# Six feed-forwards of a six-layer block: high and low activations as one operand of 512 columns, halves summed on reading, up tiles of full depth

## The reference, cut to what matters

```
gu = x @ w_gate_up;  gate, up = gu[:, :FF], gu[:, FF:]          # layers 0 to 3
y  = (silu(gate) * up) @ w_down
u  = x @ ffn_w_up;   u = causal_conv(u, taps of 3, bias)        # layers 4 and 5
y  = (silu(u[:, :FF]) * u[:, FF:]) @ ffn_w_down
```

## Time and profile before

| what | value |
|---|---|
| median of 3 runs | 2353.83 us (2352.62 to 2354.62) |
| profiled execution | 2353.8 us, span 2352.0 us, mean granted clock 0.998 |
| TensorE matmul, weight load | 98%, 88% of the span, 15272 of each |
| VectorE, ScalarE, GpSimd | 62%, 56%, 14% |

### The profile page before, as it was taken

How to read it: one execution, slowest core, us unless ns; L and a number is a source line. 1 busy time by engine, 2 the same in 40 slices (tenths; PEclk the granted TensorE clock), 3 DMA queues, 4 the chain that set the end, 5 groups by cost and what they waited for, 6 DMA issues and landing times.

```text
span 2352.0 us, 36560 instructions
## 1 busy us (share of the span) xinstructions
PE 2308.6 (98%) x15272; PEld 2067.4 (88%) x15272; DVE 1453.5 (62%) x2217; ACT 1305.4 (56%) x1958; POOL 330.6 (14%) x307
## 2 busy tenths in 40 slices
PE   7999999999999999999999999999999999999999
PEld 5799978888899888998789989899899898998998
DVE  6655555546645546546764567575677686765875
ACT  5554465555544556445564467565665675655654
POOL 0100032212100313001010002343000013530000
PEclk9999999999999999999999999999999999999999
DMA  6255443333455534555345544444455453444553
GB/s 266 90 212 183 179 178 138 141 134 126 179 190 187 197 141 157 196 182 203 113 173 186 194 178 148 144 162 162 179 187 189 175 184 126 162 164 160 201 193 126
DMA packets 58180, 398.92 MB, mean 170 GB/s; under 512 B 6816, under 2 KB 7072, under 8 KB 11680
## 3 DMA queue, kind: packets, MB, share of 16 engines
q1 hardware_dynamic: 56864, 393.75, 46.7%
q10 hardware_dynamic: 1152, 2.83, 0.3%
HBM read 395.51 MB, written 1.05 MB: 169 GB/s over the span
## 4 chain that ended last, share of the span: by engine, by line
PE 82%; DVE 9%; ACT 6%; POOL 2%; issue 1%; DMA 0%; SPq 0%; ACTq 0%; DVEq 0%; POOLq 0%
PE b L1280 12%; PE b L1282 12%; PE b L1281 12%; PE b L1178 12%; PE b L1179 12%; PE b L1180 12%; PE b L1183 5%; DVE wlo L1931 4%; PE b L1187 4%; ACT whi L1581 2%; ACT b L1577 1%; DVE xb L2229 1%; PE b L1246 1%; PE b L1247 1%; ACT S L1578 1%
## 5 line engine op out<-in xcount | busy, mean ns | idle before, releaser
L1931 DVE TENSOR_TENSOR wlo<-raw,whi 128x2048 fp32r<-128x2048 f32 x362 | 845.1, 2339 | 446.4 <-ACT whi L1581 446.1
L1581 ACT ACTIVATE whi<-raw 128x2048 fp32r<-128x2048 f32 x362 | 690.5, 1913 | 426.2 <-PE b L1282 221.9
L1280 PE MATMUL b<-xh,whi 128*128 128x256 f32 x2560 | 723.9, 283 | 1.0 <-DVE wlo L1931 0.7
L1282 PE MATMUL b<-xh,wlo 128*128 128x256 f32 x2560 | 712.4, 278 | 0.0
L1281 PE MATMUL b<-xl,whi 128*128 128x256 f32 x2560 | 711.6, 278 | 0.0
L1280 PEld LDWEIGHTS b<-xh,whi 128*128 128x128 f32 x2560 | 480.3, 188 | 5.6 <-DVE wlo L1931 3.3
L1281 PEld LDWEIGHTS b<-xl,whi 128*128 128x128 f32 x2560 | 481.4, 188 | 1.9
L1282 PEld LDWEIGHTS b<-xh,wlo 128*128 128x128 f32 x2560 | 481.1, 188 | 0.0
L1178 PE MATMUL b<-whi,xh 128*128 128x512 f32 x640 | 262.9, 411 | 1.5 <-DVE wlo L1931 1.5
L1178 PE MATMUL b<-whi,oh 128*128 128x512 f32 x656 | 259.0, 395 | 0.6 <-DVE ol L2220 0.6
L1179 PE MATMUL b<-wlo,oh 128*128 128x512 f32 x656 | 256.1, 390 | 0.0
(11 more groups left out here) (238 smaller groups left out, 2904.2 us busy)
## 6 DMA issues: line engine op xcount, KB each, us to landing
raw<-in_w SPq DMA_DIRECT2D x362, 1024.0 KB, 4.8
gt<-in_rows SPq DMA_DIRECT2D x8, 512.0 KB, 4.0
bt<-in_rows SPq DMA_DIRECT2D x8, 512.0 KB, 4.9
abq<-in_rows ACTq DMA_DIRECT2D x2, 768.0 KB, 6.3
x<-in_x SPq DMA_DIRECT2D x1, 1024.0 KB, 6.6
bc<-in_rows SPq DMA_DIRECT2D x4, 256.0 KB, 5.0
out<-x SPq DMA_DIRECT2D x4, 256.0 KB, 2.0
msk<-in_masks SPq DMA_DIRECT2D x1, 768.0 KB, 21.3
```

The costliest lines, as they stand in the source:

```text
L1280: pe.matmul(out, wh[:, k, cs], ah[:, kk, :], start=kk == 0 and s == 0, stop=False, skip_group_check=True)
L1282: last = pe.matmul(out, wl[:, k, cs], ah[:, kk, :], start=False, stop=final and k == 3, skip_group_check=True)
L1581: return ac.activation(out, i, ACT.Copy)
L1931: ve.tensor_tensor(B.wlo[r][:, :], B.raw[r][:, :], B.whi[s][:, :], ALU.subtract).then_inc(sem["loV"], 1)
```

## The change

The up projection of n = 1 to 10 is rebuilt in all six feed-forwards; n = 0 stays as it was.

- A tile of up weights holds the full depth (8 blocks) for 128 columns of gate and 128 of up (`deep` in the plan), so it fills two banks alone: `up_out` writes gate and up of column tile s into banks 4, 5 (s = 0) or 6, 7 (s = 1), every round.
- xh and xl become one tile `xa`, for each block 256 columns of the high part and then 256 of the low. One matmul moves all 512 past the high weights into the whole bank; a second moves the 256 high columns past the low weights into the first half (`deep` on TensorE). The value wanted is the sum of the bank's halves.
- f < 4: VectorE sums the halves by a reduction over pairs, gate into `us`, up into `hf` (`sum_gate`, `sum_up`); silu reads `us`; a multiply follows.
- f = 4, 5: ScalarE copies the second half into `us`, VectorE adds the first (`sum_both`); taps read `us` (`tap_sum`, `taps_sum`).
- Reading goes by one column tile (`middle(n, s)`) instead of two; the transposes of n = 0 stand one yield earlier, and `unturned` stands ahead of n = 1.
- `xa` starts 8 words behind the old start of xh, all x use it, and the tiles behind it stay where they were.

```
+    def deep(name, layer, n):
+        for s in range(2):
+            plan.append(("d", name, layer, 2 * n + s))
...
-            if n < NFF:
-                cols("w_gate_up", i, [256 * n, FF + 256 * n])
+            if n == 0:
+                cols("w_gate_up", i, [0, FF])
+            elif n < NFF:
+                deep("w_gate_up", i, n)
...
+    def up_out(self, f, n, s, name, layer):
+
+        w = self.tile(("d", name, layer, 2 * n + s))
+        for part in range(2):
+            self.bank(("deep", f, n, s, part), UPS[s][part])
+            for half in range(2):
+                self.step("deep", f, n, s, part, half, w)
+                if part and half:
+                    self.gone_by_bank(w, ("deep", f, n, s, 1))
+                yield
+        self.let_go(w)
...
-
-        def middle(n, raw):
-            if raw:
-                self.step("unturned", f)
-                yield
-                yield
-                for s in range(2):
-                    self.bank(("col", ("up", f, 0), s), UPS[1][s])
-                    self.step("turned_up", f, s)
-            yield from acts(f, n)
+        acts, parts = (self.gated, self.summed) if f < 4 else (self.convolved, self.shifted)
+
+        def first():
+            yield
             for s in range(2):
-                self.counts("hhi", (f, n, s))
-                self.step("hhi", f, n, s)
-                if s:
-                    yield
+                self.bank(("col", ("up", f, 0), s), UPS[1][s])
+                self.step("turned_up", f, s)
+            yield from acts(f)
             for s in range(2):
-                self.counts("hlo", (f, n, s))
-                self.step("hlo", f, n, s)
+                self.counts("hhi", (f, 0, s))
+                self.step("hhi", f, 0, s)
+            yield
+            for s in range(2):
+                self.counts("hlo", (f, 0, s))
+                self.step("hlo", f, 0, s)
+
+        def middle(n, s):
+            yield from parts(f, n, s)
+            yield
+            self.counts("hhi", (f, n, s))
+            self.step("hhi", f, n, s)
+            yield
+            self.counts("hlo", (f, n, s))
+            self.step("hlo", f, n, s)

         for n in range(NFF + 2):
             if n == 0:
                 self.drive(self.tok_out(("up", f), up, layer, (0, FF), a, True, PAIRS[0]))
+                self.flush()
+                self.step("unturned", f)
+                self.pre.append(first())
             elif n < NFF:
-                keys = [("c", up, layer, (256 * n, FF + 256 * n), h) for h in range(2)]
-                self.drive(self.col_out(("up", f, n), keys, ("x", a), ((0, 2), (1, 3)), UPS[(n + 1) % 2]))
-            if n < NFF:
-                self.flush()
-                self.pre.append(middle(n, n == 0))
+                for s in range(2):
+                    self.drive(self.up_out(f, n, s, up, layer))
+                    self.flush()
+                    self.pre.append(middle(n, s))
...
+    def summed(self, f, n, s):
+        self.step("sum_gate", f, n, s)
+        self.counts("silu", (f, n, s))
+        self.step("silu_sum", f, n, s)
+        yield
+        self.counts("gate", (f, n, s))
+        self.step("sum_up", f, n, s)
+
+    def shifted(self, f, n, s):
+        for part in range(2):
+            self.counts("half", (f, n, s, part))
+        self.step("sum_both", f, n, s)
+        self.counts("cva", (f, n, s))
+        self.step("tap_sum", f, n, s)
+        yield
+        self.counts("cvv", (f, n, s))
+        self.step("taps_sum", f, n, s)
+        self.counts("silu", (f, n, s))
+        self.step("silu2", f, n, s)
+        yield
+        self.counts("gate", (f, n, s))
+        self.step("gate2", f, n, s)
...
+    def deep(f, n, s, part, half, w):
+        b, m = use["deep", f, n, s, part]
+        weight_ready(w)
+        source_ready(("x", 2 * f + 1), half)
+        if half == 0:
+            p.wait_ge(f"empty{b}", m)
+        wh, wl = B.deep_of(w)
+        cs = slice(128 * part, 128 * part + 128)
+        for k in range(4 * half, 4 * half + 4):
+            pe.matmul(B.bank[b][:, :], wh[:, k, cs], B.xa[:, 512 * k:512 * k + 512], start=k == 0, stop=False,
+                      skip_group_check=True)
+            last = pe.matmul(B.bank[b][:, 0:256], wl[:, k, cs], B.xa[:, 512 * k:512 * k + 256], start=False,
+                             stop=k == 7, skip_group_check=True)
+        if half:
+            last.then_inc(sem[f"full{b}"], 1)
...
+    def silu_sum(f, n, s):
+        b, m = use["deep", f, n, s, 0]
+        a.wait_ge(f"empty{b}", m + 1)
+        act(B.sg[:, s, :], B.us[:, s, :], ACT.Silu).then_inc(sem["silu"], 1)
...
+    def sum_both(f, n, s):
+        for part in range(2):
+            b, m = use["deep", f, n, s, part]
+            a.wait_ge(f"full{b}", m + 1)
+            copy(B.us[:, part, :], B.bank[b][:, 256:512]).then_inc(sem["half"], 1)
+
+    def tap_sum(f, n, s):
+        i = f - 4
+        fw, fb = B.colp(f"fw{i}"), B.colp(f"fb{i}")
+        a.wait_ge("hlo", mark["hlo", (f, n - 1, s)])
         for j, to in enumerate((B.sg, B.hf)):
             c = 22 * j + 2 * n + s
-            last = act(to[:, s, :], B.bank[b][:, 256 * j:256 * j + 256], ACT.Identity, bias=fb[:, c:c + 1],
-                       scale=fw[:, 3 * c + 2:3 * c + 3])
+            b, m = use["deep", f, n, s, j]
+            a.wait_ge(f"empty{b}", m + 1)
+            last = act(to[:, s, :], B.us[:, j, :], ACT.Identity, bias=fb[:, c:c + 1], scale=fw[:, 3 * c + 2:3 * c + 3])
         last.then_inc(sem["cva"], 1)
...
+    def add_halves(out, f, n, s, part):
+        b, m = use["deep", f, n, s, part]
+        v.wait_ge(f"full{b}", m + 1)
+        ve.tensor_reduce(out, B.bank[b][:, :].rearrange("p (h n) -> p n h", h=2), AX.X,
+                         ALU.add).then_inc(sem[f"empty{b}"], 1)
+
+    def sum_gate(f, n, s):
+        add_halves(B.us[:, s, :], f, n, s, 0)
+
+    def sum_up(f, n, s):
+        v.wait_ge("hlo", mark["hlo", (f, n - 1, s)])
+        add_halves(B.hf[:, s, :], f, n, s, 1)
+        b, m = use["deep", f, n, s, 1]
+        v.wait_ge(f"empty{b}", m + 1)
+        v.wait_ge("silu", mark["silu", (f, n, s)])
+        ve.tensor_tensor(B.hf[:, s, :], B.hf[:, s, :], B.sg[:, s, :], ALU.mult).then_inc(sem["gate"], 1)
+
+    def sum_both(f, n, s):
+        for part in range(2):
+            b, m = use["deep", f, n, s, part]
+            us = B.us[:, part, :]
+            v.wait_ge("half", mark["half", (f, n, s, part)])
+            ve.tensor_tensor(us, B.bank[b][:, 0:256], us, ALU.add).then_inc(sem[f"empty{b}"], 1)
...
+    def taps_sum(f, n, s):
+        fw = B.colp(f"fw{f - 4}")
+        v.wait_ge("cva", mark["cva", (f, n, s)])
+        for j, to in enumerate((B.sg, B.hf)):
+            c = 22 * j + 2 * n + s
+            last = convolve(to[:, s, :], B.us[:, j, :], fw[:, 3 * c:3 * c + 3], 3)
+            if j == 0:
+                last.then_inc(sem["cvv"], 1)
+            else:
+                B.tap_i = v.mine(last)
...
-        self.acts = sb("xh", [128, 2056], F32R), sb("xl", [128, 2104], F32R)
+        sb("lead", [128, 8])
+        self.xa = sb("xa", [128, 4096], F32R)
+        sb("rest", [128, 56])
...
+        self.us = self.E[2][:, :].rearrange("p (s n) -> p s n", s=2)
...
     def act(self, x):
-
-
-        places = (8, 0) if x in (0, 2, 4, 6) else (0, 24)
-        return [a[:, at:at + 2048].rearrange("p (k n) -> p k n", k=8) for a, at in zip(self.acts, places)]
+        both = self.xa[:, :].rearrange("p (k h n) -> p k h n", k=8, h=2)
+        return both[:, :, 0, :], both[:, :, 1, :]
+
+    def deep_of(self, w):
+        return [b.rearrange("p (k n) -> p k n", k=8) for b in (self.whi[w % NHL][:, :], self.wlo[w % NRAW][:, :])]
```

More of the change, by code:

```diff
@@ L146, in stream_plan @@
         for n in range(NFF + 2):
[L147 to L148 removed]
+            if n == 0:
+                cols("ffn_w_up_2", l, [0, FF])
+            elif n < NFF:
+                deep("ffn_w_up_2", l, n)
             if n >= 2:
@@ L771, in ffn, with gated, convolved @@
         finish()
-    def gated(self, f, n):
+    def gated(self, f):
         for s in range(2):
-            self.counts("silu", (f, n, s))
-        self.step("silu", f, n)
+            self.counts("silu", (f, 0, s))
+        self.step("silu", f)
         yield
-        self.step("gate", f, n)
+        self.step("gate", f)
         yield
-    def convolved(self, f, n):
+    def convolved(self, f):
         for s in range(2):
[L783 to L794, removed]
+            self.counts("cva", (f, 0, s))
+            self.step("tap", f, s)
         yield
         for s in range(2):
-            self.counts("gate", (f, n, s))
-        self.step("gate2", f, n)
-        yield
+            self.counts("cvv", (f, 0, s))
+            self.step("taps", f, s)
+        for s in range(2):
+            self.counts("silu", (f, 0, s))
+            self.step("silu2", f, 0, s)
+        yield
+        for s in range(2):
+            self.counts("gate", (f, 0, s))
```

(30 more changed lines are left out.)

41 lines of the change are left out of this document (21 added, 20 removed).

## The result

Measured: 2364.63 us median (2363.59 to 2364.85, 4 runs) against 2353.86 us for the kernel before on the same chip, ratio 1.0045, 95% interval 1.0028 to 1.0063. The forecast was 2352.3. The profiled execution's span is 2363.0 us against 2352.0, 11.0 more.

A forecast was written before the change was run, and what follows sets the result against it. It took the rate at which TensorE starts matmuls as the bound. Terms -9.0 + 5.6 - 3.3 - 0.4 + 5.6 = -1.5 us, from 2353.8 to 2352.3 us; range 2340 to 2361.

The forecast's parts named there:

- Wide operand: Up projections, rounds 1 to 10, six layers: three matmuls (351.4 ns) become a pair at 346.7 ns, gaining 9.0 us.
- rival D: Up projections: 512 columns pay the slow 233.1 ns behind a 256; loss 3.3 us instead of 9.0 won, 2364.6; chance 0.08.
- the rule weighed there: Up projections: a warm matmul takes N/2.4 + 2.5 ns, so merging two saves 2.5 ns, 4.8 us in all; total 2356.5.
- Same tile elsewhere: Second-stage mixers: streaming x loses 5.6 us, holding x stationary gains 3.3; feed-forwards' first projections gain 0.4 us.
- Reading, gated layers: Gated feed-forwards: two reductions of about 0.7 us join each half round on VectorE, hidden by TensorE, costing nothing.
- Convolution, steady state: Feed-forwards with convolution: VectorE's chain of 15.45 us a round keeps up with TensorE's 16.56, 1.1 us to spare.
- Rival C: Rounds 2 to 10 of the last two feed-forwards: VectorE's chain becomes the bound, 16 us more, 2368; chance 0.14.
- Convolution, start: First rounds of feed-forwards 4 and 5: TensorE waits for banks, 2.8 us a layer, 5.6 us for two.

The follow-up runs named there:

- groups of eight: Changed kernel with all eight 512-column matmuls of a bank first, then its eight of 256: 2354.18 us.
- early sums: Changed kernel with the sums of round 1's second half moved ahead of the first half's high and low copies, feed-forwards 4 and 5 only: 2358.88 us.
- the fastest among them: Changed kernel with sums of round 1 moved earlier and a tile's first part eight wide then eight narrow, its second the reverse: 2347.63 us.
- the tile off the grid: Changed kernel with the activation tile starting 32 bytes earlier, 32 bytes past a multiple of 64: 2360.93 us.
- narrow first: Changed kernel with the 256-column matmul before the 512-column one in each pair, lengths still alternating: 2363.9 us.
- groups of eight off the grid: Changed kernel with eight wide then eight narrow matmuls and the activation tile 32 bytes past a multiple of 64: 2367.9 us.
- groups of four: Changed kernel with four 512-column matmuls first, then four of 256, in every half of a group: 2359.23 us.
- the wide one split: Changed kernel with each 512-column matmul written as two of 256 with the same weights: 2374.51 us.

## Why the prediction was wrong, step by step

**Wide operand: the step that failed.** The pair was priced at 346.7 and measured 352.8. Both parts of the sum were right as settled intervals, but in the steady rounds neither length settles at its own: wide ones take 232 to 241, narrow ones 113 to 120. The prediction said that no row alternates them, and then took the sum of two settled rows as the middle. The size is that of rival D (353.1; its total of 2364.6 is the measured one), its mechanism in part: the wide matmuls pay 236 on the mean while narrow ones stand between them, but not always, as the pattern of 347 ns shows. The argument against D, that the down rows settle at 226.7, was true and beside the point: they have 24 matmuls to settle in. With the alternation taken out (groups of eight) a pair takes 348.3 and the kernel 2354.2. That this is near the forecast is partly luck, since the other errors below nearly cancel. The runs show that the loss shrinks as the lengths change less often; why the steady rounds fall into the dear pattern, and not into the one whose sum is the forecast 346.7, stays open. By the rule weighed there (the Trainium skill, TensorE: Matmul & The Clock Gate, "Back-to-back issue gap") a matmul's gap depends on its columns alone; here the same 512 columns measure 226.7, 233 or 241 ns. The section gives that formula for a single matmul, and for a stream with weight loads a measured 131 ns at 512 columns, which is farther still from this trace; the prediction used the formula for a stream.

**Same tile elsewhere.** Right in each interval: the mixers' projections at 120.0 (96 in 11.52 us, before 11.24), the token projections at 227 from 233. The net of +1.9 was too dear (it came out at -0.4): in each mixer the first projection lost 0.84 us, and three quarters of a microsecond came back in the state stage, where a wait of 0.5 us on GpSimd is gone.

**Reading, gated layers.** Right. The reduction over 512 values took 0.69 us (0.7 forecast), and no wait shows. VectorE works 10.98 us a round, not 12.2: the 9.4 that the forecast started from holds the low parts of two rounds, since the window of the earlier trace rows begins ahead of one pair and ends behind the next.

```profile
L2298 DVE TENSOR_REDUCE S<-b 128x256 f32<-128x512 f32 x160 | 108.7, 687 | 39.8 <-PE b L1346 39.8
```

**Convolution, steady state.** Right: no wait in later rounds. Rival C is out.

**Convolution, start.** Right in place and size, and the run with early sums shows the mechanism of the longest stop. By the distances between starts TensorE stops three times in layer 5, for 0.13, 0.39 and 2.14 us, and in layer 4 for 0.17, 0.29 and 2.15; forecast were 0.1, 0.45 and 2.2. Only the longest is listed as a wait (1.9). These are the second and the third stop of layer 5, each between the start of a narrow matmul and the next wide one, where 0.12 us is usual (the wide one then takes another 0.08 longer):

```profile
2195.14 0.28 PE L1346 MATMUL b<-xa,wlo 128*128 128x256 f32 x1
2195.57 0.47 PE L1344 MATMUL b<-xa,whi 128*128 128x512 f32 x1
...
2201.08 0.28 PE L1346 MATMUL b<-xa,wlo 128*128 128x256 f32 x1
2203.26 0.47 PE L1344 MATMUL b<-xa,whi 128*128 128x512 f32 x1 [1.90 <-DVE S L2317]
```

What the sum lacked is the clock. Behind the longest stop in layer 4 it fell. These are windows of layer 4, behind the wait, and one at the same place of layer 5:

```profile
1718.70:1720.40 1.70, 1.55 (x9) 1.39 (x10) 0.81 (x3) 1.60 (x3) 0.00 (x0) 0.97 0.95 371
1720.40:1723.60 3.20, 3.20 (x12) 2.72 (x12) 2.87 (x6) 2.57 (x5) 0.00 (x0) 0.50 0.23 97
...
2203.10:2206.00 2.90, 2.74 (x15) 2.44 (x16) 1.94 (x6) 2.79 (x3) 0.00 (x0) 1.00 0.77 322
```

TensorE had waited 1.9 us, worked 1.55 us at a granted clock of 0.97, and then 3.2 us at 0.50, the level of 1.2 GHz. It costs 1.5 us, the difference between 23.80 us in layer 4 and 22.30 in layer 5 above.

**Not in the sum.** In before, the last rows of feed-forward 4 waited 0.6 us for a low part and the transposes behind them 1.3 us for the norm; after the change neither waits (1.9 of the -2.3). I read only that the last low part would be just in time, and didn't ask what the end of a layer waits for now. Which of the edits took the waits away wasn't tried. The other is attention, in the last section.

## What to carry to other kernels

Price a new mix of matmul shapes by a row that has the same mix; two settled intervals need not add up when the lengths alternate. Where a tile needs two lengths, try each in a group of eight or more, and lay the groups so that equal lengths meet; here that helped with the tile on a multiple of 64. When an operand is moved, look at the interval of every user at both lengths: here the same 32 bytes speed one up and slow the other down. Before a cheaper pattern is put down to an edit, look whether the kernel without it already shows that pattern somewhere.

## What the runs showed that I had not expected

**GpSimd beside VectorE.** Attention of layers 1 and 2, which the change doesn't touch, lost 1.5 and 1.4 us, most of it in a wait for the rotary multiplies on GpSimd. The same instructions of layer 2: first the changed kernel, GpSimd and VectorE, then the run with early sums, which has the same code there and no such wait.

```profile
814.67 2.38 POOL L2643 TENSOR_TENSOR rtmp<-xn,ss 128x64 f32<-128x64 f32 x1
817.12 2.49 POOL L2645 TENSOR_TENSOR xn<-xn,cc 128x128 f32<-128x128 f32 x1
...
814.57 4.73 DVE L2010 TENSOR_TENSOR wlo<-raw,whi 128x2048 fp32r<-128x2048 f32 x2 [1.01 <-ACT whi L1643]
```
```profile
813.52 0.32 POOL L2651 TENSOR_TENSOR rtmp<-xn,ss 128x64 f32<-128x64 f32 x1
813.92 0.47 POOL L2653 TENSOR_TENSOR xn<-xn,cc 128x128 f32<-128x128 f32 x1
...
815.61 4.73 DVE L2018 TENSOR_TENSOR wlo<-raw,whi 128x2048 fp32r<-128x2048 f32 x2 [3.19 <-ACT whi L1649]
```

A multiply of 0.32 or 0.47 us takes 2.38 or 2.49 when it starts while a conversion runs. The Trainium skill (GPSIMD Engine Reference, "Key points") says that GpSimd shares its SBUF interfaces with VectorE and contends with instructions that read two inputs from SBUF; the trace agrees, 2.38 against 0.32 us. Whether the wait comes is a matter of a microsecond: the changed kernel has it in both layers (1.3 and 1.1 us), and so have six of the other runs, the fastest among them; early sums has it in layer 1 alone (1.4), the tile off the grid once (0.8). So 1 to 3 us of any run here hang on the phase of the weight conversions, and a difference of that size outside the feed-forwards says nothing on the edit. No run held the conversions back, so that it is the phase is read from the traces, not tried.

**The clock after a wait.** Waits of 1.9 us at the same place were followed by half speed in one of two layers (the changed kernel and the tile off the grid: layer 4; narrow first: layer 5), in both (groups of eight off the grid) or in neither (groups of four, groups of eight, the wide one split). That is one execution of each, and 5 of 14 waits. What decides stays open.
